# Softmax rounds of two attention branches merged at three stage boundaries of a two-block model on one core

## The chip, the cores and the metric

The kernel is one program on one core of a Trainium2 chip. A core has five engines, each with its own instruction queue: TensorE (PE, matrix products and transposes into PSUM), VectorE (DVE), ScalarE (ACT), GpSimd (POOL) and SyncE (SP, which here issues the DMAs). They meet through semaphores. PSUM has eight banks of 128 x 512 float32. The metric is the time of one execution in microseconds; lower is better. Before the change three runs gave a median of 3460.84 us (3460.06 to 3464.72).

## The reference

Two blocks follow each other on x of 512 positions by 1024 channels. The first is a feed-forward, a Fourier/state-space mixer and another feed-forward; the change doesn't touch it. The second block, two layers deep, is where the change is. Each layer computes, in float32:

```python
h = rmsnorm(x, attn_norm[l]); z = h @ w_in[l]
(qA, kA, vA, fA, qB, kB, vB, qI, kI, wI, qC, kC, vC, gC, qD, kD, vD, gates) = split(z)
yA = forgetting_attention(qA, kA, vA, fA, forget_bias[l])            # 8 heads, causal
yB = dsa_attention(rope(qB), rope(kB), vB, rope(qI), rope(kI), wI)   # 8 heads, top-k keys
yC = head_groupnorm(retention(rope(qC), rope(kC), vC)) * silu(gC)    # 8 heads, no softmax
yD = sliding_window_gqa(rope(qD), rope(kD), vD, sinks)               # 8 heads, window 128
branch = einsum('bsnc,ncd->bsnd', stack([yA, yB, yC, yD]), w_branch[l])
x = x + sum(sigmoid(gates) * branch, axis=2) @ w_out[l]
x = x + (silu(a) * b) @ w_down[l]        # a, b: depthwise conv of rmsnorm(x) @ w_up[l]
```

## The kernel before, in words

**Projections.** Every product with a weight is done in three matmuls of 512 columns (L1486 to L1488: high part by high part, high by low, low by high), so that float32 accuracy is kept. An output tile of 128 channels by 512 positions is 8 such triples, 24 matmuls, in one PSUM bank. Its weights come by DMA (one "chunk"); at the step `begin`, which stands ahead of each tile, ACT makes the high part of the chunk after next (L1837) and POOL the low part (L2776, L2777).

**Rope tiles.** The tiles qb, qd, kc and qc go through a rotary embedding. ACT copies the tile out of PSUM (L1931, step `evac`), SP issues four DMAs of 32 partitions each that swap the halves (L1417), DVE multiplies the swapped copy by the sine (L2387, `rope` part 0), POOL multiplies the straight copy by the cosine (L2792), and DVE adds the two (L2391, `rope` part 1).

**Rounds.** The softmax branches A, B and D each have 16 units w: t runs over 4 pairs of heads, j over 4 blocks of 128 queries (`PAIRS`). Unit w has logits of 128 (j+1) keys per head (A and B) or of 128 or 256 (D). `heads(kind)` lays a branch out in 20 rounds. Round k holds `s1` and `s1v` of unit k, `sp2` of unit k-2, `s2` of unit k-3, and in every other round `s3`:

- `s1`: PE computes the logits of the unit's two heads (L1733 and L1744 for A, L1738 for B and D), one PSUM bank each.
- `s1v`: DVE adds the mask and takes the row's maximum (L2659, L2666), which moves the logits into one of six SBUF tiles `Lg`; ACT takes the exponential there (L2154).
- `sp2`: DVE divides by the sum (L2676, L2677).
- `s2`: PE transposes the probabilities (L1756, one bank per head); ACT copies them out (L2170).
- `s3`: PE multiplies two units by V (L1773, banks 6 and 7); each second one ends in ACT's copy into `yf` (L2180).

After a branch's 20 rounds stand four `takey` steps: ACT writes the high part `yh` of the branch's result (L2221), DVE the low part `yl` (L2742). The next branch's product with `w_branch` (`br` tiles) reads them. Branch C has no softmax; its steps are `c1` (logits, and a product with a decay table on DVE, L2721), `c2` (product with V), `rn1` and `rn2` (norm).

**What sets the order.** `schedule()` writes one list of steps, and every engine takes its own instructions from it in that order. A stage is a run of projection tiles (`fore()`), into which `weave` puts rounds: each matmul triple of 512 columns costs 0.64, the cost times the rate is added up, and at each whole number one round goes in. What is left at the stage's end goes behind it. The stages of a layer's attention, with the branch whose rounds they carry: gt and qb tiles (A, rate 0.325); qd, kc, vc and br tiles (B, 0.245); qc, gt, br (D, 0.245); gc, gt, br (C, 0.35). A branch's rounds end within its own stage.

**Banks.** `number()` deals banks 0 to 5 out in turn as the steps come. PE waits at a bank's next use until its last reader is done (`bank_of`). A rope tile's bank is freed by ACT's `evac`, a logits bank by DVE's L2659, a transposes bank by ACT's L2170.

## Time and profile before

| | |
|---|---|
| median of 3 runs | 3460.84 us |
| the profiled execution's own time | 3463.49 us |
| its span, first to last instruction | 3462.2 us |
| PE busy | 3381.9 us, 98% of the span |
| DVE / ACT / POOL busy | 47% / 41% / 38% |
| mean granted TensorE clock | 0.994 of full |

PE is busy almost all the time, so a microsecond counts only where it makes PE wait or gives it work. A matmul of 512 columns is listed with 0.39 us but the next starts 0.23 us later: they overlap. Layer 0's rounds run from 1450 to about 1880 us of the span, layer 1's from 2511 to about 2945 us.

### The profile page before, as it was taken

What the parts mean: (1) busy time and instruction counts of PE and PEld (TensorE: products, weight loads), DVE (VectorE), ACT (ScalarE), POOL (GpSimd) and SP (SyncE); (2) the same over time, 40 slices, a digit from 0 to 9 for tenths busy, and PEclk for the clock granted to TensorE, in tenths of its full rate; (3) what the DMA queues carried; (4) which work ended last, traced back from release to release, by engine and by line L of the source; (5) the groups of instructions that cost most, each with busy time, mean ns of one, the idle gap of its engine ahead of it and who ended that gap; (6) DMA issues with size and microseconds to landing.
All of it is one profiled execution on the core that took longest, in us unless ns stands there. A gap on an engine that the chain in (4) does not pass through costs nothing.

```text
span 3462.2 us, 44383 instructions
## 1 busy us (share of the span) xinstructions
PE 3381.9 (98%) x16880; PEld 2716.5 (78%) x16880; DVE 1610.9 (47%) x3080; ACT 1418.3 (41%) x2397; POOL 1321.3 (38%) x1032
## 2 busy tenths in 40 slices
PE   7999999998999999999999999999999999999998
PEld 5888899885688887777776888887877776788887
DVE  6856566666520115755542343232865452344142
ACT  4223455654532224354443344343354453344242
POOL 2776200000044443434433444444534333444443
PEclk9999999999999999999999999999999999999999
DMA  7566455221123323223222222323323222223332
GB/s 305 201 217 218 128 185 170 87 88 49 49 91 92 104 86 103 89 68 98 80 91 73 91 92 89 101 89 115 100 74 95 79 75 92 91 80 96 99 96 87
DMA packets 117716, 373.26 MB, mean 108 GB/s; under 512 B 15360, under 2 KB 16256, under 8 KB 117120
## 3 DMA queue, kind: packets, MB, share of 16 engines
q1 hardware_dynamic: 115024, 364.74, 32.5%
q10 hardware_dynamic: 2480, 5.68, 0.5%
q8 instruction: 135, 2.21, 0.3%
q14 instruction: 77, 0.63, 0.1%
HBM read 356.73 MB, written 2.10 MB: 104 GB/s over the span
## 4 chain that ended last, share of the span: by engine, by line
PE 87%; DVE 5%; ACT 3%; issue 2%; DMA 2%; POOL 1%; SPq 1%; ACTq 0%; DVEq 0%; POOLq 0%
PE ps L1486 26%; PE ps L1488 25%; PE ps L1487 25%; PE ps L1756 2%; PE ps L1773 1%; PE ps L1738 1%; PE ps L1529 1%; ACT b L1837 1%; DVE b L2278 1%; PE ps L1733 1%; DVE b L2446 1%; PE ps L1546 1%; PE ps L1797 1%; PE ps L1808 1%; DMA b<-b 1%
## 5 line engine op out<-in xcount | busy, mean ns | idle before, releaser
L1486 PE MATMUL ps<-b,b 128*128 128x512 f32 (+1 forms) x4688 | 1768.5, 377 | 27.3 <-DVE b L2267 6.0
L1488 PE MATMUL ps<-b,b 128*128 128x512 f32 (+1 forms) x4688 | 1733.9, 370 | 0.0
L1487 PE MATMUL ps<-b,b 128*128 128x512 f32 (+1 forms) x4688 | 1732.5, 370 | 0.0
L2776 POOL TENSOR_TENSOR b<-b,b 128x512 fp32r<-128x512 f32 (+1 forms) x494 | 629.1, 1273 | 2082.3 <-ACT b L1837 2078.8
L1486 PEld LDWEIGHTS ps<-b,b 128*128 128x128 f32 x4688 | 883.9, 189 | 216.0 <-issue 52.2
L1488 PEld LDWEIGHTS ps<-b,b 128*128 128x128 f32 x4688 | 883.6, 188 | 153.7
L1487 PEld LDWEIGHTS ps<-b,b 128*128 128x128 f32 x4688 | 884.6, 189 | 148.5 <-issue 5.5
L1837 ACT ACTIVATE b<-b 128x1024 fp32r<-128x1024 f32 (+1 forms) x618 | 603.8, 978 | 318.7 <-PE ps L1488 306.5
L2777 POOL TENSOR_TENSOR b<-b,b 128x512 fp32r<-128x512 f32 (+1 forms) x494 | 650.0, 1316 | 0.0
L1901 ACT ACTIVATE b<-b 128x512 fp32r<-128x512 f32 (+1 forms) x110 | 64.8, 589 | 347.7 <-DVE b L2322 244.7
L2408 DVE CUSTOM_DVE_ANT_0 b<-b,b,b 128x1024 bf16<-128x1024 f32 x108 | 188.2, 1742 | 39.7 <-DMA b<-in_ada 32.2
L2313 DVE SCALAR_TENSOR_TENSOR b<-ps,b,b 128x511 f32<-128x511 f32 x88 | 66.0, 750 | 248.7 <-ACT b L1891 248.7
L2278 DVE TENSOR_TENSOR b<-b,b 128x1024 fp32r<-128x1024 f32 (+2 forms) x124 | 138.9, 1123 | 81.1 <-ACT b L1837 80.7
L2322 DVE TENSOR_TENSOR b<-ps,b 128x512 f32<-128x512 f32 (+1 forms) x66 | 39.6, 599 | 277.4 <-PE ps L1488 271.1
L2659 DVE CUSTOM_DVE_ANT_0 b<-ps,b 128x128 f32<-128x128 f32 (+2 forms) x192 | 87.2, 454 | 157.9 <-PE ps L1756 131.3
L2154 ACT ACTIVATE b<-b,b 128x128 f32<-128x128 f32 (+2 forms) x192 | 102.2, 534 | 97.0 <-DVE b L2666 68.7
L1976 ACT ACTIVATE b<-b 128x512 f32<-128x512 f32 (+1 forms) x112 | 64.2, 582 | 186.3 <-DVE b L2341 60.1
L2170 ACT ACTIVATE b<-ps 128x128 f32<-128x128 f32 (+2 forms) x192 | 69.0, 409 | 150.6 <-PE ps L1756 150.2
L1891 ACT ACTIVATE b<-ps,b 128x512 f32<-128x512 f32 x88 | 68.6, 779 | 97.1 <-PE ps L1488 96.8
L2336 DVE TENSOR_TENSOR b<-b,ps 128x512 f32<-128x512 f32 x32 | 22.0, 687 | 185.3 <-PE ps L1488 185.3
L2328 DVE TENSOR_TENSOR b<-b,b 128x512 fp32r<-128x512 f32 (+1 forms) x110 | 70.2, 638 | 80.8 <-ACT b L1901 80.8
L2677 DVE TENSOR_SCALAR b<-b,b 128x128 f32<-128x128 f32 (+2 forms) x192 | 100.9, 526 | 6.8
(240 smaller groups left out, 2378.6 us busy)
## 6 DMA issues: line engine op xcount, KB each, us to landing
b<-in_w SPq DMA_DIRECT2D x454, 512.0 KB, 3.4
b<-in_ada SPq DMA_DIRECT2D x86, 512.0 KB, 5.6
b<-in_w SPq DMA_DIRECT2D x80, 384.0 KB, 3.1
b<-in_w SPq DMA_DIRECT2D x80, 320.0 KB, 2.9
b<-b SPq DMA_DIRECT2D x160, 64.0 KB, 2.0
b<-in_const SPq DMA_DIRECT2D x24, 256.0 KB, 3.8
b<-in_x SPq DMA_DIRECT2D x2, 1024.0 KB, 11.3
out<-b SPq DMA_DIRECT2D x8, 256.0 KB, 2.0
```

The source lines that it names most:

```text
L1486: pe.matmul(out, a[0], b[0], start=first, stop=False, **kw)
L1487: pe.matmul(out, a[0], b[1], start=False, stop=False, **kw)
L1488: return pe.matmul(out, a[1], b[0], start=False, stop=last, **kw)
L1837: act.activation(whi[j % NS][:, 0:nk * w], raw[j % NR][:, 0:nk * w], ACT.Copy).then_inc(up("hi", j), 1)
L2154: m = act.activation(q[:, 0:hi - lo], q[:, 0:hi - lo], ACT.Exp, bias=sx[:, 1:2], accum_out=sx[:, 2:3])
L2278: dve.tensor_tensor(wlo[j % NS][:, 0:nk * w], raw[j % NR][:, 0:nk * w], whi[j % NS][:, 0:nk * w].bitcast(F32), ALU.subtract).then_inc(up(" ...
L2328: dve.tensor_tensor(hl[:, i % 11, 0:N], q[:, 0:N], hh[:, i % 11, 0:N].bitcast(F32), ALU.subtract).then_inc(up("hl", f, i), 1)
L2408: m = dve.tensor_tensor_reduce(spare[:, :], ada_slot(x)[:, :], cb[:, w, :], 1.0, pv("ada_b", p), ALU.mult, ALU.add, mod[:, p, w:w + 1])
L2659: dve.tensor_tensor_reduce(Lg[u % 6][:, 0:w], PB[st["bank"][p]][:, 0:w], mk, 0.125, -3e38, ALU.add, ALU.max, sx[:, 0:1]).then_inc(up("t1", ...
L2677: dve.tensor_scalar(q, q, sx[:, 4:5], None, ALU.mult).then_inc(up("pr", a, l, u), 1)
L2776: pool.tensor_tensor(wlo[j % NS][:, 0:h], raw[j % NR][:, 0:h], whi[j % NS][:, 0:h].bitcast(F32), ALU.subtract)
L2777: then(pool.tensor_tensor(wlo[j % NS][:, h:2 * h], raw[j % NR][:, h:2 * h], whi[j % NS][:, h:2 * h].bitcast(F32), ALU.subtract), "lop", j)
```

## The change

The last four rounds of A no longer stand in A's stage. `chained` joins them one by one with the first four of B, which run in B's stage, and the four `takey` steps of A come behind the fourth joint round. The same is done from B to D, and from D to C (there with `c1` and `c2`). As 16 rounds a stage are now spread over the same tiles, the rates are lower (0.27, 0.2, 0.2; 0.36 for C). Unit u of B uses the `Lg` tile 2 further in the ring of six, unit u of D 4 further, so that a branch goes on where the one before stopped, and waits for that one's unit 26 + u. The first two of C's decay tables are fetched at the ninth round of D's 16 and no longer at C's first step. `rn1` and `rn2` become lists, since `chained` adds lists.

```diff
--- before.py
+++ after.py
@@ -578,6 +578,11 @@
                 out.append(step)
             return out
 
+        def chained(rest, rounds, o):
+            out = [x + y for x, y in zip(rest, rounds)]
+            out[-1] += [do("takey", l=l, o=o, t=t) for t in range(4)]
+            return out + rounds[len(rest):]
+
         def select(j):
             return ([do("sq", l=l, j=j, h=h) for h in (0, 2)] + [do("sm", l=l, j=j)]
                     + [do("st", l=l, j=j, r=r) for r in range(16)] + [do("sl", l=l, j=j)])
@@ -618,17 +623,21 @@
                 t = F.fm("gt", m - m // 3, "gt", H, L, o=0, l=l)
                 F.settle()
                 F.step("evac", t=t)
-        S += weave(F, rounds, 0.325) + [do("takey", l=l, o=0, t=t) for t in range(4)]
+        S += weave(F, rounds[:16], 0.27)
+        rounds = chained(rounds[16:], heads("B"), 0)
         F = fore()
         F.rope("qd", 4, "qd", ver=H, l=l)
         F.rope("kc", 4, "kc", ver=H, l=l)
         F.tm("vc", 2, "vc", H, 4, l=l)
         branch(F, 0, 0)
-        S += weave(F, heads("B"), 0.245) + [do("takey", l=l, o=1, t=t) for t in range(4)]
+        S += weave(F, rounds[:16], 0.2)
+        rounds = chained(rounds[16:], heads("D"), 1)
         F = fore()
         F.rope("qc", 4, "qc", ver=H, l=l)
         branch(F, 1, 1)
-        S += weave(F, heads("D"), 0.245) + [do("takey", l=l, o=2, t=t) for t in range(4)]
+        rounds[8].append(do("decay", l=l))
+        S += weave(F, rounds[:16], 0.2)
+        rest = rounds[16:]
         F = fore()
         F.lin("gc", 4, "gc", H, L, l=l)
         branch(F, 3, 2)
@@ -637,8 +646,8 @@
             B.append([do("c2", l=l, w=w) for w in ((k - 3, k - 2) if k % 2 and k > 2 else ())]
                      + [do("c1", l=l, w=w) for w in (k,) if w < len(PAIRS)])
             if k >= 2 and (k - 2) % 4 == 3:
-                B += [do("rn1", l=l, t=(k - 2) // 4), do("rn2", l=l, t=(k - 2) // 4)]
-        S += weave(F, B, 0.35)
+                B += [[do("rn1", l=l, t=(k - 2) // 4)], [do("rn2", l=l, t=(k - 2) // 4)]]
+        S += weave(F, chained(rest, B, 2), 0.36)
         F = fore()
         branch(F, 2, 3)
         S += weave(F, [do("takey", l=l, o=3, t=t) for t in range(4)], 0.6) + [do("mg", l=l, i=i) for i in range(6, 8)]
@@ -1305,9 +1314,9 @@
         "A": (Q1, K1, V1, lambda h: h // 2, lambda h: 64 * h), "B": (Q2, KB_, VB_, lambda h: 1 - h % 2, lambda h: 0),
         "D": (Q1, KD_, VD_, lambda h: (h // 4) ^ (h % 2), lambda h: 64 * (h // 4))}
 
-    def before6(u):
-
-        return max(x for x in range(32) if x % 6 == u % 6)
+    def logits(a, u):
+
+        return Lg[(u + 2 * "ABD".index(a)) % 6]
 
     def p_slots(p):
         return [Q[10], Q[5]] if p in (1, 2, 3) else [Q[10], Q[5], Q[4], Q[3]]
@@ -1434,13 +1443,15 @@
                     at.wait_ge(*n("fo1", x - 2))
                 a = CAT[("cl", "sl")[x // 4]] + 512 * (x % 4)
                 sp.dma_start(tabs[x % 2], CN[:, a:a + 512]).then_inc(s[f"d_tab{x % 2}"], 16)
+            elif k == "decay":
+                for h in range(2):
+                    at.wait_ge(*n("s1", "B", st["l"], 31))
+                    sp.dma_start(dh[h], CN[:, CAT["dh"] + 512 * h:CAT["dh"] + 512 * h + 512]).then_inc(s[f"d_dh{h}"], 16)
             elif k == "c1":
                 l, (t, i) = st["l"], PAIRS[st["w"]]
                 if i == 0:
-                    for h in ((0, 1, 2, 3) if t == 0 else (2 * t + 2, 2 * t + 3) if t < 3 else ()):
-                        if h < 2:
-                            at.wait_ge(*n("s1", "B", l, 31))
-                        elif h < 4:
+                    for h in ((2, 3) if t == 0 else (2 * t + 2, 2 * t + 3) if t < 3 else ()):
+                        if h < 4:
                             at.wait_ge(*n("s1", "D", l, 31))
                         else:
                             at.wait_ge(*n("c1v", l, 8 * (h // 2 - 2) + 6 + h % 2))
@@ -1753,7 +1764,7 @@
                     b = bank_of(st["bank"][p])
                     at.wait_ge(*n("pr", a, l, u))
                     for i in range((hi - lo) // 128):
-                        m = pe.transpose(b[:, 128 * i:128 * i + 128], Lg[u % 6][:, 128 * i:128 * i + 128], ident)
+                        m = pe.transpose(b[:, 128 * i:128 * i + 128], logits(a, u)[:, 128 * i:128 * i + 128], ident)
                     m.then_inc(up("tp", a, l, u), 1)
                     freed[st["bank"][p]] = ("pt", a, l, u)
             elif k == "s3":
@@ -2149,7 +2160,7 @@
                 lo, hi = span(a, j)
                 for p in range(2):
                     h, u = 2 * t + p, 2 * st["w"] + p
-                    q, sx = Lg[u % 6], stat[:, u, :]
+                    q, sx = logits(a, u), stat[:, u, :]
                     at.wait_ge(*n("mx", a, l, u))
                     m = act.activation(q[:, 0:hi - lo], q[:, 0:hi - lo], ACT.Exp, bias=sx[:, 1:2], accum_out=sx[:, 2:3])
                     if a == "D":
@@ -2652,11 +2663,11 @@
                     if u >= 6:
                         at.wait_ge(*n("tp", a, l, u - 6))
                     elif a != "A":
-                        at.wait_ge(*n("tp", {"B": "A", "D": "B"}[a], l, before6(u)))
+                        at.wait_ge(*n("tp", {"B": "A", "D": "B"}[a], l, 26 + u))
                     else:
                         at.wait_ge(*n("sc", l, 3, 3))
                     at.wait_ge(*n("s1", a, l, u))
-                    dve.tensor_tensor_reduce(Lg[u % 6][:, 0:w], PB[st["bank"][p]][:, 0:w], mk, 0.125, -3e38, ALU.add, ALU.max,
+                    dve.tensor_tensor_reduce(logits(a, u)[:, 0:w], PB[st["bank"][p]][:, 0:w], mk, 0.125, -3e38, ALU.add, ALU.max,
                                              sx[:, 0:1]).then_inc(up("t1", a, l, u), 1)
                     at.wait_ge(*n("t1", a, l, u))
                     if a == "D":
@@ -2669,7 +2680,7 @@
                 lo, hi = span(a, PAIRS[st["w"]][1])
                 for p in range(2):
                     u = 2 * st["w"] + p
-                    q, sx = Lg[u % 6][:, 0:hi - lo], stat[:, u, :]
+                    q, sx = logits(a, u)[:, 0:hi - lo], stat[:, u, :]
                     at.wait_ge(*n("ex", a, l, u))
                     if a == "D":
                         own(dve.tensor_tensor(sx[:, 2:3], sx[:, 2:3], sx[:, 3:4], ALU.add))
@@ -2716,7 +2727,7 @@
                     if u >= 6:
                         at.wait_ge(*n("c2", l, u // 2 - 3))
                     else:
-                        at.wait_ge(*n("tp", "D", l, before6(u)))
+                        at.wait_ge(*n("tp", "D", l, 26 + u))
                     at.wait_ge(*n("c1", l, u))
                     dve.tensor_tensor(Lg[u % 6][:, 0:w], PB[st["bank"][p]][:, 0:w], dh[h % 4][:, 0:w], ALU.mult).then_inc(
                         up("c1v", l, u), 1)
```

Two places show how the order moves, both in B's stage of layer 0. On DVE, from the rope steps of tile qd0 to the work of B's unit 1 (two heads of 256 logits: L2659 and L2666 before); before:

```order
L2387 TENSOR_TENSOR b_161<-b_161,b_154 128x512
L2659 ISA b_74,b_175<-ps,b_167 128x256
L2659 ISA b_175 128x1
L2666 TENSOR_SCALAR b_175<-b_175 128x1
L2659 ISA b_75,b_175<-ps,b_167 128x256
L2659 ISA b_175 128x1
L2666 TENSOR_SCALAR b_175<-b_175 128x1
L2391 TENSOR_TENSOR b_161<-b_161,b_67 128x512
```

And now (L2398 and L2402 are the rope steps, L2687 and L2688 the division of A's unit 15, L2670 and L2677 unit 1 of B):

```order
L2398 TENSOR_TENSOR b_161<-b_161,b_154 128x512
L2402 TENSOR_TENSOR b_161<-b_161,b_67 128x512
L2687 RECIPROCAL b_175<-b_175 128x1
L2688 TENSOR_SCALAR b_172<-b_172,b_175 128x512
L2687 RECIPROCAL b_175<-b_175 128x1
L2688 TENSOR_SCALAR b_73<-b_73,b_175 128x512
L2670 ISA b_76,b_175<-ps,b_167 128x256
L2670 ISA b_175 128x1
L2677 TENSOR_SCALAR b_175<-b_175 128x1
L2670 ISA b_77,b_175<-ps,b_167 128x256
L2670 ISA b_175 128x1
L2677 TENSOR_SCALAR b_175<-b_175 128x1
```

Unit 1's maxima stood between the two rope steps of qd0; now they stand behind both and behind A's division.

On ACT, the same round of 512-column logits (unit 3 of B) up to the copy of tile qd3, which is L1931 before; before:

```order
L2154 ACTIVATE b_172,b_175<-b_172,b_175 128x512
L2154 ACTIVATE b_73,b_175<-b_73,b_175 128x512
L2170 ACTIVATE b_173<-ps 128x2x128
L2170 ACTIVATE b_174<-ps 128x2x128
L2154 ACTIVATE b_74,b_175<-b_74,b_175 128x128
L2154 ACTIVATE b_75,b_175<-b_75,b_175 128x128
L1931 ACTIVATE b_68<-ps 128x512
```

And now (L1942 is the copy, L2165 the exponential, L2181 the copy of transposes, L2191 that into `yf`, L2232 `yh`):

```order
L2191 ACTIVATE b_158<-ps 128x512
L2181 ACTIVATE b_173<-ps 128x128
L2181 ACTIVATE b_174<-ps 128x128
L2165 ACTIVATE b_74,b_175<-b_74,b_175 128x512
L2165 ACTIVATE b_75,b_175<-b_75,b_175 128x512
L2232 ACTIVATE b_159<-b_158 128x512 x4
L1942 ACTIVATE b_68<-ps 128x512
```

The four `yh` copies stood ahead of B's first round before; now they, and unit 3's own exponentials, stand right ahead of the copy of tile qd3.

More widely, with the step list of the changed kernel beside that of the old: rounds 0 to 4 of B's stage now stand each behind the last matmul of tiles qd0, qd1, qd2, qd3 and kc0, ahead of the tile's own `evac`, and rounds 5 to 7 one triple ahead of the last of kc1, kc2 and kc3. Before they stood at steps of these tiles that drifted: behind the 7th triple of qd0, the 5th of qd1, the 4th of qd2, the 2nd and the 8th of qd3, the 7th of kc0, the 5th of kc1, the 4th of kc2, the 2nd and 8th of kc3. In qc0 to qc3 and the tile behind them it is the same. The banks of qd0, qd1, qd2, qd3, kc0 and kc1 are now 2, 1, 0, 5, 4 and 3, and each is written again by the round behind the next tile: the round behind kc0 puts its logits into banks 5 and 0, the one in kc1 into 4 and 5, the one in kc2 into 3 and 4. Of a layer's attention, 94 places where small matmuls interrupt the triples become 82.

## Rows read from the trace of the kernel before

**Rows 1.** The page, busy time of PE, share, instructions.

```profile
PE 3381.9 (98%) x16880; PEld 2716.5 (78%) x16880; DVE 1610.9 (47%) x3080; ACT 1418.3 (41%) x2397; POOL 1321.3 (38%) x1032
```

**Rows 2.** Stretches: us, busy (instructions) PE, PEld, DVE, ACT, POOL; clock; DMA; GB/s.

```profile
1550.00:1620.00 70.00, 67.28 (x358) 49.95 (x355) 40.81 (x113) 33.35 (x79) 37.25 (x27) 1.00 0.32 94
1705.00:1755.00 50.00, 48.44 (x258) 35.95 (x257) 27.50 (x110) 26.86 (x80) 20.62 (x15) 1.00 0.23 72
1795.00:1815.00 20.00, 18.84 (x83) 11.81 (x82) 5.02 (x11) 3.34 (x5) 7.57 (x6) 1.00 0.43 147
2610.00:2875.00 265.00, 259.88 (x1410) 195.78 (x1405) 135.06 (x424) 123.10 (x307) 112.63 (x83) 1.00 0.29 87
```

**Rows 3.** Timeline of PE, B's stage: start, duration, instruction [idle before].

```profile
1576.96 0.39 PE L1487 MATMUL ps<-b,b 128*128 128x512 f32 x1
1577.19 0.39 PE L1488 MATMUL ps<-b,b 128*128 128x512 f32 x1
1577.51 0.63 PE L1738 MATMUL ps<-b,b 64*128 64x128 f32 x4
1579.77 0.87 PE L1756 MATMUL ps<-b,b 128*128 128x128 f32 x4 [1.63 <-DVE b L2677]
...
1585.38 0.87 PE L1773 MATMUL ps<-b,b 128*64 128x256 f32 x8
...
1587.44 0.48 PE L1486 MATMUL ps<-b,b 128*128 128x512 f32 x1
...
1592.05 0.92 PE L1738 MATMUL ps<-b,b 64*128 64x384 f32 x4 [0.27 <-ACT b L1931]
...
1598.71 1.73 PE L1773 MATMUL ps<-b,b 128*64 128x256 f32 x16
1600.38 1.13 PE L1738 MATMUL ps<-b,b 64*128 64x512 f32 x4
```

**Rows 4.** Timeline of ACT, B's stage and the `takey` ahead.

```profile
1551.03 2.18 ACT L2221 ACTIVATE b<-b 128x512 fp32r<-128x512 f32 x4
...
1579.30 0.19 ACT L2154 ACTIVATION_READ_ACCUMULATOR b<-b,b 128x1 f32 x1
...
1582.69 0.58 ACT L1931 ACTIVATE b<-ps 128x512 f32<-128x512 f32 x1
...
1591.42 0.58 ACT L1931 ACTIVATE b<-ps 128x512 f32<-128x512 f32 x1
...
1598.57 0.58 ACT L1931 ACTIVATE b<-ps 128x512 f32<-128x512 f32 x1
```

**Rows 5.** Timeline of DVE, the same stretch.

```profile
1557.14 3.57 DVE L2742 TENSOR_TENSOR b<-b,b 128x512 fp32r<-128x512 f32 x4
...
1576.91 0.68 DVE L2659 CUSTOM_DVE_ANT_0 b<-ps,b 128x512 f32<-128x512 f32 x1
...
1587.11 0.69 DVE L2387 TENSOR_TENSOR b<-b,b 128x512 f32<-128x512 f32 x1 [3.81 <-DMA b<-b]
1589.07 0.69 DVE L2391 TENSOR_TENSOR b<-b,b 128x512 f32<-128x512 f32 x1 [1.26 <-POOL b L2792]
1589.67 0.42 DVE L2659 CUSTOM_DVE_ANT_0 b<-ps,b 128x256 f32<-128x256 f32 x1
...
1591.58 0.49 DVE L2677 TENSOR_SCALAR b<-b,b 128x512 f32<-128x512 f32 x1
...
1596.45 0.55 DVE L2659 CUSTOM_DVE_ANT_0 b<-ps,b 128x384 f32<-128x384 f32 x1
```

**Rows 6.** Waits from 1795 to 1815 us: us in total, times, longest.

```profile
DVE b L2721 <- DMA b<-in_const: 7.6, 2, 6.9
...
PE ps L1797 <- DVE b L2367: 1.2, 1, 1.2
```

**Rows 7.** Stretches of the first block, columns as in rows 2.

```profile
790.00:795.00 5.00, 1.39 (x5) 0.98 (x4) 4.89 (x7) 0.00 (x0) 0.00 (x0) 0.85 0.35 105
795.00:800.00 5.00, 5.00 (x15) 4.32 (x15) 2.57 (x7) 0.00 (x0) 0.00 (x0) 0.50 0.00 0
```

## Prediction

> **What bounds the kernel now.** I read the page first: PE is busy 98% of the span [rows 1]. So only two things can move the time: PE's waits inside the three stages that the change touches, and the work PE itself is given. Next I took the stretches where a branch begins [rows 2]. The first is the rope part of B's stage in layer 0: PE idles 70 - 67.28 = 2.7 us. D's start idles 1.6, C's start 1.2, together 5.4; layer 1 from B's start to C's start idles 5.1. About 10.5 us, 0.3% of the time, is all that better overlap could give back. The timeline of PE then says what it waited for at B's start: the divided probabilities of B's first units, from DVE (1.63 us in one wait), and once the copy of a rope tile, from ACT (0.27 us) [rows 3]. So I read ACT and DVE around those waits [rows 4, 5]. There is a chain that goes round once per rope tile. ACT copies a tile at 1582.69. The swapped halves are back at 1587.11, when DVE does the sine. POOL's cosine makes DVE wait until 1589.07, when it adds. From 1589.67 DVE takes the maxima of a 256-wide unit, ACT its exponentials, and ACT copies the next tile only at 1591.42. That is 8.73 us from copy to copy, and right behind it stands PE's 0.27 us wait for that copy.
>
> PE needs less than this for a tile. Triples run at 0.23 us a matmul (1576.96 to 1577.19), so 24 take 5.5 us, and a round's small matmuls some 2 us: 2.06 us from 1585.38 to 1587.44 with 8 products, 256-wide logits and 6 transposes [rows 3]. Together 7.6 us. The kernel before gets away with it because its rounds drift through the tiles: the round in kc1 stands ahead of the last rope step, and ACT's next copy comes 7.15 us after the one before (1591.42 to 1598.57) [rows 4].
>
> **What the change does to that chain.** Sixteen rounds at rate 0.2 come every 1 / 0.2 = 5 units of cost; a tile costs 8 x 0.64 = 5.12. So the round falls on the same place in every tile, its last matmul, and on DVE it stands behind both rope steps of the tile before. Every tile of qd and kc now has the 8.73 us pattern, never the short one. I work out the copies of the eight tiles, with 0 at the start of round 0 on PE, when tile qd0 is done.
>
> - From copy to the start of the maxima: 1589.67 - 1582.69 = 6.98 us [rows 4, 5].
> - From there to the next copy, by width: 256: 1.75 (to 1591.42); 384: 2.12 (1596.45 to 1598.57); 512: 1576.91 to 1579.49, 2.5; 128: 1.36, an estimate one step of 0.4 below 256.
> - In rounds 0 and 1 DVE first divides A's units 14 and 15, an estimate of 2 x 0.6 = 1.2 us from the 0.49 us row [rows 5].
> - In round 3 ACT makes A's four high parts ahead of the copy. They took 1551.03 to about 1553.1: 2.1 us [rows 4].
>
> Copy 0 is at 4.2: qb3's copy comes about 0.2 behind that tile's end and its rope 6.98 later, which is 1.7 us into round 0, as qd0 takes 5.46; then 1.2 and 1.36. Then: copy 1 at 4.2 + 6.98 + 1.2 + 1.75 = 14.2; copy 2 at + 9.1 = 23.3; copy 3 at + 6.98 + 2.5 + 2.1 = 34.9; copy 4 at + 8.34 = 43.3; copy 5 at + 8.73 = 52.0; copy 6 at + 9.1 = 61.1; copy 7 at + 9.5 = 70.6.
>
> PE's own needs: 5.46 a tile, and for rounds 0 to 7 about 1.1, 2.3, 1.9, 3.1, 1.1, 2.1, 1.8, 3.0, from the rows for 8 products (0.87), 16 products (1598.71 to 1600.38, 1.67), logits (0.63, about 0.7, 0.92, 1.13 by width) and transposes at about 0.11 each [rows 3]. PE may write a tile's bank again 0.6 us after its copy starts, and it does so in the round behind the next tile. Going through: round 1 starts at 6.6, no wait. Round 2 at 14.4 waits 0.4 for copy 1. Round 3 at 22.2 reaches its logits at 23.9, as copy 2 frees the bank: none. Round 4 is there at 30.9 and needs qd3's bank, free at 35.5: 4.6. Round 5 reaches its logits at 42.3, free at 43.9: 1.6. Round 6: 50.8 against 52.6, 1.8. Round 7: even. The next two rounds, over vc, still wait for DVE, which is behind copy 7: about 1.7 and 0.8. Sum 10.9 us, where the kernel before has 2.7: **+8.2 us in each layer**.
>
> D's stage has four rope tiles. The same sums with 256-wide units and the two sink exponentials (about 0.4 more a round) give copies at 2.8, 13.1, 22.3, 33.6 and 42.3. Round 4 waits 4.5 us for qc3's bank and the next 1.8 for gt0's: 6.3 against 1.6, **+4.7 us**.
>
> C's stage has no rope. There the early fetch of the decay tables takes away DVE's wait of 6.9 us at C's first unit and PE's 1.2 behind it [rows 6]; in layer 1 about half of that. The joint rounds put A-like work next to `c1` on a DVE that is busy 5 of 20 us there [rows 2], so I take **-0.9 us**. The fetch stands on SP's queue amid D's weights; it waits for nothing, and 256 KB at a load of 0.23 of the DMA engines is hidden.
>
> Interruptions of the triples: 94 become 82 in each layer. Going in costs 0.32 instead of 0.23 us (1577.19 to 1577.51) [rows 3], coming out about as much, nothing where transposes stand first. 12 x 0.11 = **-1.3 us**. The shift in `Lg` costs nothing: it gives the same distance of three units between a tile's uses at a branch's edge as inside one. A's stage gets slacker rounds (0.27 for 0.325), with little idle time to win.
>
> Sum: 8.2 + 4.7 - 0.9 - 1.3 = 10.7 a layer, 21.4 in both. Against the profiled execution's own 3463.5 that is 3484.9. The median of the runs stands 2.7 lower, so I predict **3482 us**.
>
> **Bounds.** The unknown is how late PE gets. From below: if ACT had the first copy as soon as its data allow, 1.7 us earlier, and everything not in rows went well, the stalls would be 9 and 4 us: +7 a layer. From above: DVE's operations stretch when POOL works; the 0.69 us add would be one of them. Half a microsecond more a tile is +6 a layer.
>
> **The clock.** In the first block PE was busy 1.39 us of five, and the granted clock fell to 0.85 and then to 0.50 for the next five, which held 15 matmuls [rows 7]: 2.5 us lost. A wait of 4.6 us is longer than the idle 3.6 us of that stretch. Four such waits would cost up to 10 us. But a slow PE behind round 4 only uses up the 1.6 and 1.8 us that it would wait for copies 4 and 5 anyway. I take 0 and keep up to 4. The Trainium skill ("TensorE: Matmul & The Clock Gate", Why this matters for your kernels) says that idle gaps between bursts of matmuls bring the slow clock back. By that rule alone all four waits would be followed by half speed, and the sum would be up to 3492; the trace agrees as far as its one gap goes. I give that a tenth, inside my forecast's share.
>
> **Rivals.**
> 1. Faster: the chain is not what limits. With the rounds 5.1 instead of 4.1 units apart, each division on DVE has a unit more before PE asks for its result, the waits of [rows 2] go, and so do the interruptions. For it: the longest waits at B's start are for divisions, not for copies [rows 3]. Against it: the one copy that stands in the new pattern already made PE wait. Gain: (5.3 + 1.3) x 2 = 13, or half: 3448 to 3455.
> 2. No change within 0.2% (about 7 us, what a measurement of this kernel can tell): PE's head start is larger than I think. It decides at round 4: if the four high parts and A's divisions hide in it and only later tiles stall, +3 and +1 a layer meet -2.2, which makes +3.6 in both: 3464.
> 3. Slower, but from the joint rounds alone: the `takey` steps in round 3 and 4.6 us behind them are the whole loss, about +3 us at two places in two layers, +12 less 4: 3469. This is my mechanism without its steady part.
> 4. The change does nothing because both orders wait for the same rope DMAs. The sum of waits would stay, less the interruptions: 3458.
>
> **How the numbers follow.** My forecast with rival 3: 0.71. Rival 2 with rival 4: 0.14. Rival 1: 0.15. So slower by over 0.2% 0.71, within 0.14, faster 0.15. The forecast's own range is 3468 to 3492. The range to hold 8 in 10 goes down to 3455, which leaves out most of rival 1, and up to 3492.
>
> **What would show it.** Right: in the changed profile the starts of ACT's rope copies (L1942) in B's stage lie 8.3 to 11.7 us apart in every tile, one near 11.7 at qd3; PE's logits line waits for ACT L1942, with one wait of 4 to 5 us in each B and each D stage of both layers; the rope stretch of B idles about 11 us. C's wait for `in_const` is gone. Wrong: copies 7.6 us apart, with PE not waiting for them; or idle time in these stretches under 3 us. If PE idles as said but the clock's share drops below 0.99, the clock part was too small.

## The result: 3505.4 us against 3461.1, and the profile after

Four runs of the changed kernel gave a median of 3505.43 us (3501.37 to 3506.68), four of the kernel before 3461.11 (3460.06 to 3464.72): a ratio of 1.0122, 95% interval 1.0109 to 1.0134. The change makes the kernel slower by 44 us. I had forecast slower, by 21, with 3492 as the upper end: the measured time is outside my range. Lines of the changed kernel stand 11 lower down for the same code: L1942 is ACT's rope copy, L1749 the logits of B and D, L1767 the transposes, L1497 to L1499 the triples, L2398, L2402 and L2803 sine, add and cosine.

The page's row of busy time, to be laid beside [rows 1]:

```profile
PE 3392.4 (97%) x16880; PEld 2731.6 (78%) x16880; DVE 1590.0 (45%) x3080; ACT 1414.8 (40%) x2397; POOL 1323.3 (38%) x1032
```

The profiled span went from 3462.2 to 3503.8 us, +41.6. PE is busy 10.5 us longer with the same 16880 matmuls, so it idles 31.1 us longer. The same four stretches as in [rows 2], columns as there:

```profile
1550.00:1620.00 70.00, 59.00 (x291) 42.84 (x290) 28.49 (x88) 27.89 (x64) 31.26 (x22) 0.95 0.26 78
1705.00:1755.00 50.00, 45.38 (x224) 34.11 (x223) 25.05 (x92) 25.06 (x72) 21.14 (x15) 0.93 0.26 80
1795.00:1815.00 20.00, 20.00 (x102) 14.81 (x101) 12.91 (x43) 10.59 (x30) 7.89 (x6) 1.00 0.18 65
2610.00:2875.00 265.00, 244.49 (x1334) 188.05 (x1334) 113.08 (x398) 115.13 (x290) 106.16 (x77) 0.97 0.26 78
```

B's rope stretch idles 11 us (2.7 before), D's start 4.6 (1.6), C's start not at all (1.2). The granted clock is below 1.00 in three of the four, where it was 1.00 in all. What PE waited for in layer 0's attention, with the sum, the number and the longest of the waits:

```profile
PE ps L1749 <- ACT b L1942: 11.4, 4, 4.6
PE ps L1497 <- ACT b L1942: 4.4, 1, 4.4
PE ps L1767 <- ACT b L1942: 4.1, 2, 2.8
PE ps L1829 <- ACT b L2210: 1.1, 1, 1.1
```

Before, PE waited 0.3 us in this stretch for L1931, the same copy. The waits for divisions at B's start [rows 3] are gone, and waits for the copy have taken their place. The last line, at C's first norm (`rn1`), is new. In layer 1 the longest waits are 3.2 us at round 2, 4.5 at round 4 and 5.9 at the vc tile, and 4.6 in D's stage. PE's timeline in B's stage, only the instructions with a wait, in brackets:

```profile
1558.96 0.88 PE L1767 MATMUL ps<-b,b 128*128 128x128 f32 x6 [1.34 <-ACT b L1942]
1568.91 1.09 PE L1767 MATMUL ps<-b,b 128*128 128x128 f32 x8 [2.77 <-ACT b L1942]
1590.63 0.71 PE L1749 MATMUL ps<-b,b 64*128 64x128 f32 x4 [3.96 <-ACT b L1942]
1607.68 0.92 PE L1749 MATMUL ps<-b,b 64*128 64x384 f32 x4 [1.74 <-ACT b L1942]
1617.89 1.13 PE L1749 MATMUL ps<-b,b 64*128 64x512 f32 x4 [1.12 <-ACT b L1942]
```

These are rounds 1, 2, 4, 6 and 7. Behind them a tile of vc waits 4.4 us more for the copy of kc3, the last rope tile. ACT's copies in the same stage, answering to [rows 4]:

```profile
1558.34 0.57 ACT L1942 ACTIVATE b<-ps 128x512 f32<-128x512 f32 x1
1568.28 0.58 ACT L1942 ACTIVATE b<-ps 128x512 f32<-128x512 f32 x1
1577.42 0.58 ACT L1942 ACTIVATE b<-ps 128x512 f32<-128x512 f32 x1
...
1587.92 2.17 ACT L2232 ACTIVATE b<-b 128x512 fp32r<-128x512 f32 x4
1590.00 0.57 ACT L1942 ACTIVATE b<-ps 128x512 f32<-128x512 f32 x1
...
1597.94 0.40 ACT L2165 ACTIVATE b<-b,b 128x128 f32<-128x128 f32 x1
1598.34 0.57 ACT L1942 ACTIVATE b<-ps 128x512 f32<-128x512 f32 x1
...
1607.05 0.57 ACT L1942 ACTIVATE b<-ps 128x512 f32<-128x512 f32 x1
...
1617.26 0.57 ACT L1942 ACTIVATE b<-ps 128x512 f32<-128x512 f32 x1
...
1626.72 0.58 ACT L1942 ACTIVATE b<-ps 128x512 f32<-128x512 f32 x1
```

From copy to copy: 9.9, 9.1, 12.6, 8.3, 8.7, 10.2 and 9.5 us. Each starts when the exponentials of the round (L2165) end, 0.40 us after the last one's start at 1597.94; the 12.6 holds the four high parts (L2232). The clock, in stretches with PE's busy time, granted clock, share of DMA and GB/s:

```profile
1585.00:1590.00 5.00, 1.67 (x8) 1.00 0.00 0
1590.00:1595.00 5.00, 4.37 (x17) 0.66 0.22 54
1595.00:1600.00 5.00, 4.92 (x30) 1.00 0.33 105
```

Right behind the wait of 3.96 us, which ends at 1590.63, the clock falls to half (1.2 GHz), and it is full again by 1595. In all, the clock record of the trace shows seven such half-speed stretches in the attention layers, 37.5 us long together; the kernel before has none there. At half speed the matmuls of a triple start 0.43 us apart, not 0.23 [rows 3]; these two stand in the first of the seven:

```profile
1572.23 0.63 PE L1499 MATMUL ps<-b,b 128*128 128x512 f32 x1
1572.65 0.63 PE L1497 MATMUL ps<-b,b 128*128 128x512 f32 x1
```

### The profile page after: what moved, and what is told of

The parts are those of the page before. It is cut to its first block, busy times and chain, and to the rows that moved or that the text cites. A ratio compares the mean times of both kernels' runs of the same rounds, so it can differ in the third digit from the quotient of the medians.

```text
span 3503.8 us, 44429 instructions
## 1 busy us (share of the span) xinstructions
PE 3392.4 (97%) x16880; PEld 2731.6 (78%) x16880; DVE 1590.0 (45%) x3080; ACT 1414.8 (40%) x2397; POOL 1323.3 (38%) x1032
## 4 chain that ended last, share of the span: by engine, by line
PE 84%; DVE 4%; ACT 4%; DMA 2%; issue 2%; POOL 2%; SPq 2%; ACTq 0%; DVEq 0%; POOLq 0%
PE ps L1497 25%; PE ps L1498 25%; PE ps L1499 25%; DMA b<-b 2%; SPq L1426 1%; PE ps L1767 1%; POOL b L2803 1%; PE ps L1784 1%; PE ps L1540 1%; PE ps L1749 1%; ACT b L2165 1%; DVE b L2670 1%; PE ps L1808 1%; PE ps L1744 1%; ACT b L1848 1%
## 5 line engine op out<-in xcount | busy, mean ns | idle before, releaser
L1497 PE MATMUL ps<-b,b 128*128 128x512 f32 (+1 forms) x4688 | 1771.6, 378 | 36.1 <-ACT b L1942 10.3
L1499 PE MATMUL ps<-b,b 128*128 128x512 f32 (+1 forms) x4688 | 1737.8, 371 | 0.0
L2787 POOL TENSOR_TENSOR b<-b,b 128x512 fp32r<-128x512 f32 (+1 forms) x494 | 627.5, 1270 | 2112.3 <-ACT b L1848 2109.0
L1497 PEld LDWEIGHTS ps<-b,b 128*128 128x128 f32 x4688 | 888.0, 189 | 224.0 <-issue 52.1
L1499 PEld LDWEIGHTS ps<-b,b 128*128 128x128 f32 x4688 | 887.6, 189 | 153.4
L2788 POOL TENSOR_TENSOR b<-b,b 128x512 fp32r<-128x512 f32 (+1 forms) x494 | 648.2, 1312 | 0.0
L2165 ACT ACTIVATE b<-b,b 128x128 f32<-128x128 f32 (+2 forms) x192 | 102.2, 533 | 166.2 <-DVE b L2677 123.5
L2670 DVE CUSTOM_DVE_ANT_0 b<-ps,b 128x128 f32<-128x128 f32 (+2 forms) x192 | 87.2, 454 | 178.1 <-PE ps L1767 150.3
L2181 ACT ACTIVATE b<-ps 128x128 f32<-128x128 f32 (+2 forms) x192 | 68.8, 408 | 178.3 <-PE ps L1767 178.0
L2398 DVE TENSOR_TENSOR b<-b,b 128x512 f32<-128x512 f32 x40 | 27.6, 691 | 167.1 <-DMA b<-b 167.1
```

The source lines that it names most:

```text
L1497: pe.matmul(out, a[0], b[0], start=first, stop=False, **kw)
L1499: return pe.matmul(out, a[1], b[0], start=False, stop=last, **kw)
L2165: m = act.activation(q[:, 0:hi - lo], q[:, 0:hi - lo], ACT.Exp, bias=sx[:, 1:2], accum_out=sx[:, 2:3])
L2181: act.activation(Pt[p][:, lo // 128:hi // 128, c:c + 128], PB[st["bank"][p]][:, 0:hi - lo].rearrange("p (i n) -> p i n", n=128), ACT.Copy) ...
L2670: dve.tensor_tensor_reduce(logits(a, u)[:, 0:w], PB[st["bank"][p]][:, 0:w], mk, 0.125, -3e38, ALU.add, ALU.max, sx[:, 0:1]).then_inc(up("t ...
L2787: pool.tensor_tensor(wlo[j % NS][:, 0:h], raw[j % NR][:, 0:h], whi[j % NS][:, 0:h].bitcast(F32), ALU.subtract)
```

## The experiments

Each is compared with runs of the kernel before made beside it, whose medians were 3462.4 to 3464.3 us; the ratio is what to read. Three words come back below. The ring is the chain of the prediction: ACT's copy of a rope tile, its rope steps, the maxima and exponentials of the round behind them, the next copy. The beat is one round at the same place of every rope tile. "Half speed" is time at the lower clock. The table sets out what the sections read: the ratio of times with its interval; PE's idle time in B's stage (rope tiles and vc) and D's stage (rope tiles to br), both layers added, each taken as stage length less busy time; the time at half speed in the attention layers; PE's busy time in the whole program.

| kernel | median us | ratio (95%) | idle B | idle D | half speed | PE busy |
|---|---|---|---|---|---|---|
| before | 3461.11 | | 5.5 | 3.3 | 0 | 3381.9 |
| changed | 3505.43 | 1.0122 (1.0109, 1.0134) | 30.2 | 10.3 | 37.5 | 3392.4 |
| e1_copy_first | 3480.62 | 1.0054 (1.0039, 1.0069) | 18.3 | 4.7 | 20.5 | 3387.4 |
| e2_beat_alone | 3506.73 | 1.0126 (1.0109, 1.0143) | 27.5 | 11.9 | 37.5 | 3399.1 |
| e3_old_rate_joined | 3465.44 | 1.0008 (0.9998, 1.0017) | 10.7 | 1.4 | 6.8 | 3379.1 |
| e4_high_parts_spread | 3506.25 | 1.0127 (1.0112, 1.0142) | 29.1 | 10.9 | 41.0 | 3392.3 |
| e5_copy_first_locked | 3469.94 | 1.0023 (1.0013, 1.0033) | 8.8 | 3.2 | 3.4 | 3383.1 |
| e6_mid_tile_joined | 3459.04 | 0.9988 (0.9979, 0.9997) | 6.1 | 0.3 | 10.2 | 3379.5 |
| e7_mid_tile_before | 3458.57 | 0.9987 (0.9978, 0.9997) | 3.5 | 1.8 | 0 | 3382.6 |
| e8_mid_tile_later | 3453.19 | 0.9969 (0.9956, 0.9981) | 3.9 | 0.3 | 0 | 3375.5 |
| e9_beat_later | 3501.55 | 1.0108 (1.0092, 1.0123) | 30.0 | 10.4 | 34.1 | 3389.6 |
| e10_best_spread | 3451.25 | 0.9964 (0.9952, 0.9977) | 6.2 | 0.3 | 3.4 | 3375.0 |
| e11_rope_carried | 3445.32 | 0.9948 (0.9935, 0.9960) | 0.8 | 0.3 | 0 | 3374.8 |
| e12_mid_before_decay | 3456.38 | 0.9981 (0.9972, 0.9990) | 3.4 | 1.8 | 0 | 3380.9 |

### e2_beat_alone: the rate without the joining

```diff
 (the kernel before; weave takes a rate for its first units)
-        S += weave(F, heads("B"), 0.245) + [...]
+        S += weave(F, heads("B"), 0.31, 0.2, 40.96) + [...]
-        S += weave(F, heads("D"), 0.245) + [...]
+        S += weave(F, heads("D"), 0.262, 0.2, 20.48) + [...]
```

> Edit: the kernel before, with nothing joined and no other change, but with the rate 0.2 over the rope tiles of B's stage and of D's (one round per tile, on its last matmul), and 0.31 and 0.262 behind them so that all 20 rounds stay in their stage. Theory (it is the beat of the rounds with the tiles): PE waits for ACT's rope copies from round 4 on as in the changed kernel, somewhat less since rounds 0 to 3 have no A work and no high parts: idle 6 to 9 us in B's rope stretch against 2.7, 2 to 4 at D's start, +5 to +9 a layer with the clock: 3475 us (3468 to 3484). Rival (the joint rounds and their high parts alone cost the time): 3461, within 5 us.

3507 us: the whole loss of the change, with nothing joined. I had the sign right and the size at a third. PE's waits in layer 0's attention:

```profile
PE ps L1739 <- ACT b L1932: 9.4, 5, 3.1
PE ps L1487 <- ACT b L1932: 6.2, 2, 4.4
PE ps L1757 <- ACT b L1932: 4.1, 2, 2.3
```

They are the waits of the changed kernel, by the same copy (here L1932). The lighter first rounds help little: in layer 0 the copies of qd1 and qd3 come 8.7 and 9.5 us behind the ones before them, where the changed kernel has 9.9 and 12.6, but the other turns are much as there or longer, and the idle time of the two stages together is 39.4 us against 40.5. So joining is not the cause. Its rival, that the joint rounds alone cost the time, falls.

### e3_old_rate_joined: the joining without the rate

```diff
-        S += weave(F, rounds[:16], 0.2)
+        S += weave(F, rounds[:16], 0.195, 0.245, 40.96)
...
-        S += weave(F, rounds[:16], 0.2)
+        S += weave(F, rounds[:16], 0.182, 0.245, 20.48)
```

> Edit: the changed kernel, rounds joined as there, but over the rope tiles of B's stage and of D's at the old rate 0.245, so that they drift through the tiles; behind them 0.195 and 0.182. Theory (beat): most of the loss goes, though the four high parts in joint round 3 and the fuller rounds 0 to 3 stay: idle 3 to 6 us in B's rope stretch, 1 to 3 at D's start; 3474 us (3466 to 3484). Rival (the joint rounds' work is the loss): 3495 or more.

3465 us, no different from before within its interval: with the old rate over twelve tiles a layer the loss is gone. B's stage still idles 10.7 us against 5.5, partly paid by D's (1.4 against 3.3).

### e1_copy_first and e5_copy_first_locked: only ACT's order

Both put the copy ahead of a round that falls on a rope tile's last matmul. In e1 the instructions of PE, DVE and POOL keep their order; e5 also moves rounds.

```diff
 (in weave, ahead of its loop)
+    for i in range(1, len(fore.items)):
+        s = fore.items[i][0]
+        if s is not None and s["kind"] == "evac" and s["t"]["name"] in ("qd", "kc", "qc") and fore.items[i - 1][0] is None:
+            fore.items[i - 1:i + 1] = [fore.items[i], fore.items[i - 1]]
```

> Edit: in the changed kernel, where a round falls on a rope tile's last matmul (qd, kc, qc), the tile's copy by ACT now stands ahead of the round and no longer behind it; on the other engines nothing moves. Theory (the loss comes from the ring copy - rope - maxima - exponentials - next copy, which closes because ACT's copy stands behind the round's exponentials): rounds 1 to 4 of B's stage and rounds 1 to 4 of D's no longer wait for a copy. Rounds 5 to 7 of B's stage stand a matmul earlier and keep their copy behind them, so they keep their waits (1 to 2 us each, and 4.4 us at the vc tile). PE idles 3 to 5 us in the rope stretch of B (11.0 in the changed kernel), under 1.5 at D's start (4.6); the slow clock behind round 4 goes. Time 3480 us (3472 to 3488). Rival (rope DMAs or POOL are the limit, whatever the order on ACT; or the joint rounds' added work is): the same stalls, 3500 to 3508.

Measured 3481, the number expected. The kernel has its own control in B's stage: in layer 0 PE waits for no copy up to round 5, where the copies stand first; behind kc0 the rounds stand one triple earlier with the copy behind them as before, and there round 6 waits 1.89 us (at 1600.33) and the vc tile 4.4. Two things expected did not come. At D's start PE still idles 2.1 and 2.6 us, in layer 0 for ACT's tanh of a gate tile (L1979); and behind round 4 a half-speed stretch of 3.4 us stays (from 1583.4), although the wait there is now one of 1.11 us for DVE's division. e5 then moves rounds 5 to 7 onto the last matmul too, so that all copies come first (with the `tiles` argument of e6 below, at slot 8, and the rates 0.26 and 0.196 behind the rope tiles):

> Edit: the changed kernel, in every rope tile of B's and D's stage (8 and 4) exactly one round, on the tile's last matmul, and ACT's copy of that tile ahead of the round; behind the rope tiles the rates 0.26 and 0.196. It keeps the beat and takes only ACT's order away, now in all tiles (e1_copy_first did it in those where the round fell on the last matmul). Theory (the beat costs only through the place of ACT's copy behind the exponentials): no waits for rope copies from round 5 on either, nor the 4 to 5 us at the vc tile; idle 2 to 4 us in B's rope stretch, 0 to 1 over vc, 1 to 2 at D's start: 3463 us (3455 to 3470). Rival (a second ring, over DVE: the maxima stand behind both rope steps of the tile before, which wait for the DMA): waits for DVE's maxima take their place, 3474 or more.

3470 us, at the edge of what was expected. ACT's order alone takes away some 25 us of the loss (e1), and in all tiles, with the rounds moved for it, some 35. PE's remaining waits in layer 0:

```profile
PE ps L1775 <- DVE b L2696: 2.8, 5, 1.1
PE ps L1757 <- ACT b L1983: 1.4, 1, 1.4
PE ps L1837 <- ACT b L2218: 1.1, 1, 1.1
PE ps L1757 <- DVE b L2678: 0.9, 3, 0.4
```

No line names the rope copy (L1983 is the tanh of a gate tile). The rival has its part: 3.7 us here wait for DVE's divisions (L2696) and maxima (L2678), and a round's work on DVE still stands behind both rope steps.

### e6_mid_tile_joined and e7_mid_tile_before: the same beat at another place

```diff
 (in weave; tiles and slot are new arguments)
+    units = 5.12 * tiles
+    if tiles:
+        due = (8 - slot) / 8 + 0.01
...
-        due += cost * rate
+        due += cost * (1 / 5.12 if units > 0.01 else rate)
+        units -= cost
...
-        S += weave(F, rounds[:16], 0.2)
+        S += weave(F, rounds[:16], 0.25, 8, 3)
...
-        S += weave(F, rounds[:16], 0.2)
+        S += weave(F, rounds[:16], 0.19, 4, 3)
```

> Edit: the changed kernel, rounds joined as there and exactly one round per rope tile, but behind the tile's third matmul triple instead of its last; ACT's copy stands where it did, behind the tile. Rates behind the rope tiles 0.25 and 0.19. Theory: the same beat at a place where the round's maxima stand ahead of both rope steps on DVE and its exponentials are done before the tile ends, so the ring isn't closed: idle under 3 us in B's rope stretch, under 1.5 at D's start: 3460 us (3450 to 3468). Rival (one round per tile at whatever place resonates, only drifting rounds are good; or the joint rounds cost): 3480 or more.

> Edit: as e2_beat_alone (the kernel before, nothing joined, one round per rope tile, 0.31 and 0.262 behind), but with the round behind the tile's third triple instead of its last. e2 took 3507 us. Theory: the place alone decides: 3460 us (3452 to 3468). Rival (the beat at any place, or the denser rounds behind the rope tiles, which e2 has too): 3490 or more.

3459 and 3459 us. A round in every tile is harmless, even a little better than the drifting ones, if it stands in mid-tile: e7 and e2 differ in little but five triples in the round's place, and in 48 us. That a beat is bad as such is refuted. Joining makes no difference between these two; e6 has a wait of 3 us in each layer for qd0's copy, with half speed behind it, which e7 has not.

### e4_high_parts_spread: the `takey` steps

```diff
-            out[-1] += [do("takey", l=l, o=o, t=t) for t in range(4)]
+            for t in range(4):
+                out[t].append(do("takey", l=l, o=o, t=t))
```

> Edit: the changed kernel, with the four takey steps of the branch that ends spread over joint rounds 0 to 3, one each, and no longer all behind round 3. Theory (they only lengthen one turn of the ring): the copy of tile qd3 comes 1.6 us earlier, the wait in round 4 falls from 4.0 to about 2.4, likewise in D's stage; with less slow clock -4 to -10 in both layers: 3498 us (3493 to 3503). Rival (those four steps and what follows them are the whole loss): 3482 or less.

3506 us: no gain, and both theories missed. The interval of qd3's copy fell from 12.6 to 10.8 us as foreseen, but the earlier ones grew by nearly as much (10.5 and 9.7 for 9.9 and 9.1, and 13.3 for 13.1 ahead of qd0). Each high part stands on ACT between the exponentials and the copy wherever it goes, so its 0.5 us stays in the ring. Spread over rounds, the cost on this ring was kept.

### e9_beat_later: the first copy's head start

```diff
-        S += weave(F, rounds[:16], 0.2)
+        S += weave(F, rounds[:16], 0.2, -1.0)
```

The new last argument is the initial `due` in B's stage.

> Edit: the changed kernel with its rate 0.2 and the round on the last matmul as there, but B's first joint round one rope tile later. It tests the term of the prediction that was mis-sized: how far ahead of PE the first copy is. Theory: the copy of qd0 comes at its tile's end instead of 8.2 us after it, and the ring has one turn less in the rope stretch; B's stage idles 7 to 10 us instead of 15.4 and 14.8 in the two layers: 3491 us (3485 to 3497). Rival (the turns of the ring alone set the loss, wherever it starts): 3502 or more.

3502 us, 10 more than expected: the rival's number. qd0's copy did come at once (1548.31), but qd1's only 15.0 us later. Four timelines of this kernel, first SP's queue (L1377 fetches a chunk), then POOL, ACT and DVE:

```profile
1543.79 2.41 SPq L1426 DMA_DIRECT2D b<-b  x4
1553.81 0.33 SPq L1377 DMA_DIRECT2D b<-in_w  x1
1554.24 2.41 SPq L1426 DMA_DIRECT2D b<-b  x4
```

```profile
1548.93 1.74 POOL L2803 TENSOR_TENSOR b<-b,b 128x512 f32<-128x512 f32 x1 [9.65 <-DMA b<-b]
1550.75 1.29 POOL L2787 TENSOR_TENSOR b<-b,b 128x512 fp32r<-128x512 f32 x1
1551.99 1.74 POOL L2788 TENSOR_TENSOR b<-b,b 128x512 fp32r<-128x512 f32 x1
```

```profile
1548.31 0.60 ACT L1942 ACTIVATE b<-ps 128x512 f32<-128x512 f32 x1 [3.60 <-PE ps L1499]
...
1563.28 0.58 ACT L1942 ACTIVATE b<-ps 128x512 f32<-128x512 f32 x1
```

```profile
1558.30 0.69 DVE L2398 TENSOR_TENSOR b<-b,b 128x512 f32<-128x512 f32 x1 [5.72 <-DMA b<-b]
1560.25 0.69 DVE L2402 TENSOR_TENSOR b<-b,b 128x512 f32<-128x512 f32 x1 [1.25 <-POOL b L2803]
```

The copy is done at 1548.9, but its rope DMA starts 5.3 us later, at 1554.24. Ahead of it in SP's queue stands the fetch of a chunk, which waits 7.5 us for POOL's low part (L2788, done at 1553.73); and POOL's low part stands behind the cosine of qb3, ahead of which POOL sat idle 9.65 us until that tile's rope DMA had landed. At the stage's start there is a second chain, over POOL and SP, and my sum had left it out.

### e8, e10, e11, e12: what the findings are worth

e8_mid_tile_later is e6 with B's first round one rope tile later.

```diff
 (in weave; late is a new argument)
-        due = (8 - slot) / 8 + 0.01
+        due = (8 - slot) / 8 + 0.01 - late
...
-        S += weave(F, rounds[:16], 0.25, 8, 3)
+        S += weave(F, rounds[:16], 0.29, 8, 3, 1)
```

> Edit: e6_mid_tile_joined (3459 us), with B's first joint round one rope tile later (in qd1 and no longer in qd0) and 0.29 behind the rope tiles. In e6 PE waited 2.95 us once per layer in round 1 for the copy of qd0, which stood behind round 0's exponentials, and these behind the late rope steps of qb3 on DVE; a slow stretch of the clock followed. Theory (first copy's head start): both go, PE idles under 0.7 us in B's rope stretch, clock 1.00 there: 3450 us (3446 to 3456), faster than the kernel before and than e7. Rival (the wait only moves to the next copy, or the rounds packed closer behind the rope tiles cost as much): 3457 to 3462.

3453 us, inside the interval expected, but a wait of 1.2 and 1.9 us stays in the two layers. e10 adds e4's edit and sets C's rate to 0.35:

> Edit: e8_mid_tile_later with the four takey steps spread over joint rounds 0 to 3 (as in e4) and C's rate 0.35 for 0.36. Theory: with the ring open, four high parts in one round hide as well as spread, so nothing is gained there; PE's wait of 1.1 us for C's first norm in each layer (new in the changed kernel) goes with the lower rate: -2 us against e8, 3448 us (3444 to 3456). Rival: the joint round with all four steps is a cost of its own even without the ring: -5 or more against e8.

3451 us. C's wait for its first norm is gone (1.10 us a layer, read from the profile); spreading the high parts gives nothing that these runs can tell from e8. e11 carries the rope steps of qb3 over, which takes the second chain apart:

```diff
+        carried, F.tail = F.tail, []
         S += weave(F, rounds[:16], 0.27)
         rounds = chained(rounds[16:], heads("B"), 0)
         F = fore()
+        F.tail = carried
```

> Edit: e10_best_spread (3451 us), with the two rope steps of qb3, the last tile of A's stage, carried into B's stage (behind the fifth and seventh triple of qd0, as for every other rope tile) and no longer at once behind the tile. What e9 showed: there POOL's cosine for qb3 waits for the rope DMA, POOL's low part of the next chunk stands behind it, SP's fetch of a chunk waits for that, and the rope DMA of qd0 stands behind the fetch, 5.9 us late. Theory: POOL's low part now goes ahead of the cosine, so the rope DMA of qd0 is issued at once and its add comes 6.4 to 7.5 us behind its copy (10.6 us in e8); PE's waits of 1.6 and 3.7 us for the copy of qd0 (one per layer) go: -4 to -8 us against e10, 3446 us (3442 to 3451). Rival (the late add is not what holds PE; the copy only stands behind round 0's exponentials): within 2 us of e10.

SP's queue in e11 (L1433 is the rope DMA, L1384 the fetch):

```profile
1543.46 2.41 SPq L1433 DMA_DIRECT2D b<-b  x4
1547.13 0.33 SPq L1384 DMA_DIRECT2D b<-in_w  x1
1548.65 2.41 SPq L1433 DMA_DIRECT2D b<-b  x4
```

The fetch is issued at 1547.13 and no longer keeps the rope DMA back, which follows qd0's copy (1548.0) at once. In B's rope stretch of layer 0 (columns as in [rows 2]) PE doesn't idle at all:

```profile
1542.35:1599.73 57.38, 57.38 (x291) 43.70 (x290) 33.93 (x92) 29.36 (x65) 31.65 (x24) 1.00 0.36 111
```

3445.3 us, 0.5% faster than the kernel before and 60 us faster than the changed one: the best version measured. e12 puts the early fetch of the decay tables alone into e7:

> Edit: e7_mid_tile_before (3458.6 us; nothing joined) with the early fetch of the first two decay tables alone, at D's ninth round. Theory: PE's idle time at C's start (1.14 and 1.81 us in the two layers of e7) goes: -3 us, 3456 us (3453 to 3459), which leaves e8 and e10 3 to 5 us ahead by the joint rounds. Rival (the fetch isn't what C's start waits for, PE's wait passes to another): as e7; or all that the joint rounds seemed to give was this fetch: 3452.

3456 us as expected, with C's start idle 0.00 us in both layers; from e7 the medians differ by 2.2 us, which the intervals don't part, so the profile alone shows it. What is left between e12 and e11 is 11 us; of that, 6.1 is PE's busy time (3380.9 to 3374.8, no half speed in the attention layers of either). Joining seems to pay once nothing else is in its way, but that is not shown by itself: the placement of rounds and the rope steps of qb3 differ between the two as well.

## Why the prediction was right in kind and wrong in size

The parts of the difference of 41.6 us in the span, beside the terms of the prediction:

| term | predicted, both layers | measured |
|---|---|---|
| idle in B's stage | +16.4 | +12.7 and +12.0 = +24.7 |
| idle in D's stage (rope tiles to br) | +9.4 | +3.1 and +3.9 = +7.0 |
| idle in C's stage | -1.8 | -0.1 and +0.6 = +0.5 |
| interruptions | -2.6 | -5.4 (PE's busy time, e8 less before) |
| clock | 0 | +14.8 (PE's busy time, changed less e8) |

The last two rows are taken in the attention layers alone. These lines have the length of their sixteen stretches and PE's busy time in them, for the kernel before, the changed one and e8, whose rounds are joined too and which has no half speed there:

```profile
sum 1062.68, PE 1050.93; mean PE 65.68
sum 1104.11, PE 1060.37; mean PE 66.27
sum 1052.96, PE 1045.57; mean PE 65.35
```

Two other readings give the clock's price too. PE is busy 30.7 us of the seven half-speed stretches, and half of that is 15.3 us of work lost. And e2 less e7, neither joined, the one with 37.5 us at half speed and the other with none, is 15.9 us of PE's busy time in the same stretches.

The measured terms sum to 41.6, the whole difference; what they leave out nearly cancels (outside the attention layers PE is busy 1.0 us longer and idles 0.9 less). Over the forecast's 21.4 that is 20.2 us: clock 14.8, B 8.3 and C 2.3 more; D 2.4 and interruptions 2.8 less.

**The mechanism was right.** Rounds on every tile's last matmul put the exponentials ahead of the copy (e1, e5), the ring takes 8.3 to 12.6 us where PE needs 7.6, and PE waits for the copy. The rate does it, not the joining (e2, e3), and only by that place in the tile (e6, e7). Rivals 1, 2 and 4 are out by the result, rival 3 by e2 and e4. What the prediction named as its signs came: intervals from 8.3 to 12.6 (8.3 to 11.7 forecast), a wait of 4 to 5 us at round 4 in each B and D stage of both layers (3.96, 4.6, 4.5, 4.6), 11.0 us idle in B's rope stretch, and C's wait for `in_const` gone. So did its sign that the clock part was too small: the mean granted clock is 0.989.

**The step that failed is the clock.** I took 0, since "a slow PE behind round 4 only uses up the 1.6 and 1.8 us that it would wait for copies 4 and 5 anyway". For round 5 this came true: it waits 0.0 us instead of 1.6. But I counted only the four waits at round 4 as ones that could bring half speed. All four did, 20.5 us together, and three more did that I had not counted: the one of 2.77 us at round 2 of layer 0, where I had 0.4, and the one of the vc tile in each layer (4.4 and 5.9 us), where I had two short ones for DVE. Those three bring the other 17.1 us. The 37.5 us at half speed cost PE some 15 us of busy time, more than the slack of 1.6 and 1.8 us that I set against them could take up. The rule of the Trainium skill ("TensorE: Matmul & The Clock Gate", Why this matters for your kernels) that I gave a tenth, that idle gaps between bursts of matmuls bring the slow clock back, is what the trace shows here: each of the seven stretches begins within one of these waits or less than 2 us behind it. I should have given each wait of the forecast its half-speed stretch, and taken off only the slack that stands behind it.

**B's idle time was short by 4 us a layer.** Layer 0: 15.4 against 10.9. The first copy came 8.2 us after round 0's start (1550.14), not 4.2, and the eight copies then took 68.4 us, not 66.4: 4.0 + 2.0, of which 4.5 reached PE: 2.6 in the rope stretch and 1.9 at the vc tile (4.4 where I had 2.5). The 4.0 is in DVE's timeline:

```profile
1551.40 0.69 DVE L2398 TENSOR_TENSOR b<-b,b 128x512 f32<-128x512 f32 x1 [6.03 <-DMA b<-b]
1553.34 1.82 DVE L2402 TENSOR_TENSOR b<-b,b 128x512 f32<-128x512 f32 x1 [1.25 <-POOL b L2803]
...
1555.27 1.26 DVE L2688 TENSOR_SCALAR b<-b,b 128x384 f32<-128x384 f32 x1
```

The sine came 1.8 us later behind the copy (1545.2) than the 4.4 of [rows 4, 5], the add took 1.82 us for the 0.69 of [rows 5], the divisions 0.7 more, and qb3's copy itself came 0.3 later. But this term was no lever of its own: e9 gave the copy its head start and the loss stayed, because the chain over POOL and SP took it. D's idle time I had too high by 1.2 us a layer: the round behind its qc3 tile waits 4.6 us as forecast (4.5), the next 0 and 0.7 in the two layers instead of 1.8, again behind a slow stretch.

**C** lost its wait as predicted, 1.2 us in layer 0, but the denser rounds brought a new one of 1.1 us for the first norm's ACT work, in both layers; I had no term for it. It is gone in e10 and e11, where C's rate is 0.35 again. **Interruptions** were worth more than I took: 24 fewer, and 5.4 us less busy time (e8 less before; e11 less e12 gives 5.6), some 0.2 us each and not 0.11. Nothing run here sets that apart from other effects of joining.

## What to carry to other kernels

A rate that sets interleaved work against tiles of fixed cost should be checked for where the work lands in the tile: near a whole ratio it lands in the same place every time, and a bad place is then met in every tile. The place to look for is the in-order queue on which a copy that frees a bank stands behind work that waits for the copy before it; follow the ring once round and compare it with what the busy engine needs. And where a forecast has waits of the matrix engine of a few microseconds, price half speed behind each of them before calling it hidden.

## What the runs showed of the hardware that I had not expected

DVE and POOL can shut each other out for a whole instruction. Beside DVE's rows of the section before, POOL's of the same stretch:

```profile
1553.32 1.29 POOL L2787 TENSOR_TENSOR b<-b,b 128x512 fp32r<-128x512 f32 x1
1554.57 1.74 POOL L2788 TENSOR_TENSOR b<-b,b 128x512 fp32r<-128x512 f32 x1
```

DVE's add starts at 1553.34, POOL's L2787 at 1553.32. The add ends at 1555.16, which is POOL's remaining 1.27 us and 0.55 more; alone it takes 0.69. Then POOL's L2788, begun during that add, takes 1.74 us and not 1.29, and DVE's division, begun at 1555.27, takes 1.26 and not 0.42. POOL's cosine shows it too: in the changed kernel 36 of the 40 take 1.7 to 1.8 us, and each of them starts beside DVE's sine, which the same DMA released; the other four take 1.3 us and have no sine beside them at their start. In e11 the same split is 12 and 28. The Trainium skill ("SBUF — State Buffer", SBUF: two separate sides) says that the two engines share a port pair, that whichever starts first holds it for its whole instruction, and that on DVE only certain kinds of instruction take it; the trace agrees, to within some 0.2 us a row.

The slow clock is not tied to one length of wait. In e3 a wait of 1.74 us, and in e1 and e5 one of 1.11, was followed by 3.4 us at half speed; in e8 waits of 1.2 and 1.9 us, in the kernel before one of 1.63, and in the changed kernel one of 3.22 (round 2 of layer 1, until 2650.6), were not. What decides it, no run here shows.
